# Two chunks per operation for the weighted activations of the late values, in a block with attention and product-key experts

## What is computed

```
def block(args):
    xt, et, gt = args
    u = expert_u[et]
    act = jax.nn.gelu(jnp.einsum('td,tkd->tk', xt, u), approximate=False) * gt
    return jnp.einsum('tk,tkd->td', act, expert_v[et])
```

## Time and profile before

| what | value |
|---|---|
| median of 3 runs | 1699.81 us |
| the profiled execution's own time | 1700.5 us |
| its span, first to last instruction | 1698.6 us |
| mean granted TensorE clock, share of full speed | 0.991 |
| TensorE matmuls busy | 1641.3 us, 97% |
| VectorE busy | 1375.8 us, 81% |
| ScalarE busy | 719.9 us, 42% |
| GpSimd busy | 767.5 us, 45% |
| moved by DMA | 432.17 MB, mean 254 GB/s |

### The profile page before, as it was taken

How to read it: one execution, slowest core, us unless ns; L and a number is a source line. 1 busy time by engine, 2 the same in 40 slices (tenths; PEclk the granted TensorE clock), 3 DMA queues, 4 the chain that set the end, 5 groups by cost and what they waited for, 6 DMA issues and landing times.

```text
span 1698.6 us, 24181 instructions
## 1 busy us (share of the span) xinstructions
PE 1641.3 (97%) x8700; PEld 1441.1 (85%) x8700; DVE 1375.8 (81%) x2835; ACT 719.9 (42%) x1135; POOL 767.5 (45%) x441
## 2 busy tenths in 40 slices
PE   6999999999999999999999889999999999999998
PEld 4677877877899999899999879999999988888886
DVE  7457656676688787999999589888879989888887
ACT  3356546543553534444444333333333344333334
POOL 0222222335356665656554445555555665333331
PEclk9999999999999999999999989999999999999999
DMA  8322242334143432578886999999998999999992
GB/s 331 115 100 87 105 180 88 138 123 149 39 140 116 156 126 96 205 265 340 322 316 225 385 397 378 360 370 360 356 367 328 342 399 398 398 367 376 378 357 100
DMA packets 141676, 432.17 MB, mean 254 GB/s; under 512 B 13584, under 2 KB 58640, under 8 KB 135696
## 3 DMA queue, kind: packets, MB, share of 16 engines
q1 hardware_dynamic: 88592, 265.61, 42.6%
q0 software_dynamic: 41472, 151.01, 23.4%
q10 hardware_dynamic: 11520, 14.42, 2.3%
HBM read 389.31 MB, written 41.68 MB: 254 GB/s over the span
## 4 chain that ended last, share of the span: by engine, by line
PE 68%; DVE 22%; DMA 4%; issue 3%; POOL 1%; ACT 1%; SPq 0%; DVEq 0%; ACTq 0%
PE bank L990 29%; PE bank L934 12%; PE bank L709 10%; DVE hot_j L1732 5%; PE bank L873 4%; DVE hot_i L1728 2%; PE bank L978 2%; DVE rows L1610 2%; DMA rows<-ev,idx 1%; DMA gates<-gates_scratch 1%; PE bank L735 1%; DMA gates_scratch<-stage 1%; DVE arena L1688 1%; PE bank L796 1%; DVE slots L1621 1%
## 5 line engine op out<-in xcount | busy, mean ns | idle before, releaser
L934 PE MATMUL bank<-h_split,u_split 128*128 128x352 f32 x3072 | 518.3, 325 | 8.6 <-DVE u_split L1604 6.9
L934 PEld LDWEIGHTS bank<-h_split,u_split 128*128 128x128 f32 x3072 | 496.6, 189 | 16.5 <-DVE u_split L1604 8.0
L990 PE MATMUL bank<-v_late,a_late 128*128 128x512 f32 x1440 | 326.7, 389 | 1.4 <-DVE a_late L1778 1.4
L990 PEld LDWEIGHTS bank<-v_late,a_late 128*128 128x128 f32 x1440 | 270.2, 188 | 57.7 <-issue 1.6
L609 POOL DMA_INDIRECT rows<-ev,idx x128 | 177.0, 1383 | 219.2 <-DVE row_sum L1719 192.7
L592 POOL TENSOR_TENSOR u_split<-u_raw,u_split 128x1024 fp32r<-128x1024 f32 x72 | 172.8, 2404 | 196.4 <-ACT u_split L1199 196.4
L582 POOL TENSOR_TENSOR block_split<-arena,block_split 128x1024 fp32r<-128x1024 f32 x48 | 118.1, 2464 | 305.6 <-ACT block_split L1054 305.6
L609 POOL DMA_INDIRECT rows<-eu,idx x128 | 182.6, 1427 | 145.4 <-DVE dots L1610 122.3
L990 PE MATMUL bank<-v_split,a_split 128*128 128x512 f32 x864 | 205.6, 392 | 8.6 <-DVE a_split L1778 8.6
L1208 ACT ACTIVATE gelus<-bank 128x352 f32<-128x352 f32 x128 | 59.5, 465 | 324.0 <-PE bank L934 324.0
L990 PEld LDWEIGHTS bank<-v_split,a_split 128*128 128x128 f32 x864 | 162.3, 190 | 39.4 <-issue 8.8
(11 more groups left out here) (281 smaller groups left out, 2406.0 us busy)
## 6 DMA issues: line engine op xcount, KB each, us to landing
u_raw<-euT SPq DMA_DIRECT2D x128, 512.0 KB, 7.8
v_raw<-ev SPq DMA_DIRECT2D x128, 512.0 KB, 7.4
arena<-w_blocks SPq DMA_DIRECT2D x50, 512.0 KB, 9.1
arena<-w_ada SPq DMA_DIRECT2D x12, 2048.0 KB, 8.2
gates_scratch<-stage SPq DMA_DIRECT2D x24, 1024.0 KB, 11.3
gates<-gates_scratch SPq DMA_DIRECT2D x32, 768.0 KB, 10.6
gelu_scratch<-gelus ACTq DMA_DIRECT2D x80, 176.0 KB, 3.4
gelus<-gelu_scratch SPq DMA_DIRECT2D x80, 176.0 KB, 9.4
```

The source lines that it names most:

```text
L934: last = pe.matmul(ps[6 + b][:, 0:TE], us[:, b, wp, k * P:(k + 1) * P], hs[:, xp, k, 0:TE], start=(k == 0 and q == 0), stop=(k == DC - 1 a ...
L990: last = pe.matmul(ps[2 * t + f][:], a[:, ap, t * P:(t + 1) * P], v[:, vp, f * 512:(f + 1) * 512], start=(first and q == 0), stop=True, sk ...
```

## The change

In the late values the multiplication with the gates, the rounding and the low half take two chunks (768 columns) in one operation each: `weights_pair`, `a_high_pair`, `a_low_pair`. `weights` has four slots instead of two. The operations on `v_raw` stay one per chunk, and so do SP's loads and TensorE's matmuls.

The order on VectorE becomes, for each even i: weights_pair(i+2), v_low(i+1), the row sums of chunk i, v_low(i+2), a_low_pair(i+2), the row sums of chunk i+1. On ScalarE it becomes: v_high(i+2), a_high_pair(i+2), v_high(i+3). weights_pair waits for the activations of both chunks, and each pair operation raises its semaphore by 2 when all of it is done.

```diff
-        wgt = carve(2, TD, name="weights")
+        wgt = carve(4, TD, name="weights")
...
-            a_high(NF)
+            def a_high_pair(i):
+
+                sa.wait_ge(w_ready, i + 2)
+                if i >= NF + LATE:
+                    sa.wait_ge(v_done, i - LATE + 2)
+                act_(a_late[:, i % LATE:i % LATE + 2, 0, :], wgt[:, i % 4:i % 4 + 2, :], ACT.Copy).then_inc(a_hi, 2)
+
+            a_high_pair(NF)
             v_high(NF + 1)
-            for i in range(NF, NK):
-                if i + 1 < NK:
-                    a_high(i + 1)
+            for i in range(NF, NK, 2):
                 if i + 2 < NK:
                     v_high(i + 2)
+                    a_high_pair(i + 2)
+                    v_high(i + 3)
...
-            weights(NF)
-            a_low(NF)
-            for i in range(NF, NK):
-                if i + 1 < NK:
-                    weights(i + 1)
-                    v_low(i + 1)
-                    a_low(i + 1)
+            def weights_pair(i):
+
+                if i % 4 == 0:
+                    ve.wait_ge(gt_in[i // 4 % GT], 16 * (i // 4 // GT + 1))
+                for k in (i, i + 1):
+                    ve.wait_ge(gl_in[k % RING], 16 * ((k - NF) // RING + 1))
+                if i >= NF + 4:
+                    ve.wait_ge(a_hi, i - 2)
+                if i < NF + 4:
+                    ve.wait_ge(a_hi, NF)
+                by_64 = dict(n=GROUPS // 16)
+                nv.tensor_tensor(wgt[:, i % 4:i % 4 + 2, :].rearrange("p i (n t) -> p i n t", **by_64),
+                                 gel[:, i % RING:i % RING + 2, :].rearrange("p i (n t) -> p i n t", **by_64),
+                                 gt[i // 4 % GT][:, :, i % 4:i % 4 + 2, :].rearrange("p n i t -> p i n t"), ALU.mult).then_inc(w_ready, 2)
+
+            def a_low_pair(i):
+
+                ve.wait_ge(w_ready, i + 2)
+                ve.wait_ge(a_hi, i + 2)
+                e = i % LATE
+                nv.tensor_tensor(a_late[:, e:e + 2, 1, :], wgt[:, i % 4:i % 4 + 2, :], a_late[:, e:e + 2, 0, :].bitcast(F32),
+                                 ALU.subtract).then_inc(a_split, 2)
+
+            weights_pair(NF)
+            a_low_pair(NF)
+            for i in range(NF, NK, 2):
+                if i + 2 < NK:
+                    weights_pair(i + 2)
+                v_low(i + 1)
                 for k in range(accs_before(i), accs_before(i + 1)):
+                    add_row(k)
+                if i + 2 < NK:
+                    v_low(i + 2)
+                    a_low_pair(i + 2)
+                for k in range(accs_before(i + 1), accs_before(i + 2)):
                     add_row(k)
```

## The result

The kernel became slower: 1764.84 us, the median of 4 runs (1762.38 to 1776.09), against 1700.28 us before, also the median of 4. The ratio is 1.0391, interval 1.0371 to 1.0411. The forecast was 1732 us with a range up to 1785; so the direction and the range held, but the loss was 65 us instead of 32, twice as much.

A forecast was written before the change was run, and what follows sets the result against it. TensorE bounds the late values before the change; afterwards a loop through gelu loads makes four chunks 18.1 us instead of 16.34, 17 times, 30 us, plus 1.1 us for the first pair: 1732 us, range up to 1785 us.

The forecast's parts named there:

- What bounds the kernel: Late values: one unbroken piece of TensorE work, 323.98 us, four chunks 16.34 us; the transfers, at 400 GB/s, have no slack.
- merged operations: VectorE and ScalarE in the late values: merging saves 5.6 us and 8 us, both under TensorE's 324 us, priced at nothing.
- first pair: Start of the late values: longer weights, rounding and low half start TensorE 1.1 us later, its wait growing to 2.5 us.
- The loop: Late values: weights_pair waits for a gelu load issued only after the previous turn's v_low, so each turn includes its landing.
- The turn without gates: VectorE turn with no gate load: 6.1 us alone, 7.4 us with one row fetch, upper bound 10.8 us.
- the prediction's floor: Turn without gates: VectorE's own work of two weights-sized pair operations, two v_low-sized ones and 2.4 row sums, 6.9 us.
- The turn with a gate load: 17 VectorE turns whose gelu load follows a gate load: 8.0 us alone, 10.7 us with two row fetches.
- The choice between the bounds: Turn lengths taken nearer the lone landing than the crowded one, because a loop awaiting its own loads leaves no older ones queued.
- The upper bound: Turn with a gate load at the crowded landing of 9.6 us: 12.6 us.
- TensorE as the bound: Rival for the late values: two turns stay under 16.34 us, only 1.1 us is lost, 1702 us; chance 0.24.
- As crowded as before: Rival for the late values: landings stay crowded, four chunks take 23.4 us, 1822 us in all; chance 0.17.
- TensorE's clock: Late values: idling some 2 us per four chunks might lower the clock, costing 1.7 us; nothing added, put into upper end.

## Why the prediction was right in its mechanism and half its size

- **What bounds the kernel, merged operations, first pair.** Right. The merged operations took the predicted 0.95 and 0.84 us and were worth nothing. TensorE's first late matmul waited 2.52 us, against 1.43 before (both rows are in the section on the result): 1.1 us, as worked out.
- **The loop.** Right, and shown: it goes with SP's order alone, it stays without merging, it shrinks when two links change places.
- **The turn without gates.** Predicted 7.4 us, measured 7.25, but partly by luck. The prediction added a landing with one fetch. In 12 of the 16 turns VectorE didn't wait for gelus at all, and its own work set the length, 6.4 us with two row sums and 7.8 us with three: the prediction's floor of 6.9 us.
- **The turn with a gate load.** This is the term that failed: "I take two: 8.0 + 2.6 = 10.7 us". It measured 12.55 us. By the runs, the loads alone land 1.2 us later than bytes at 400 GB/s make them (6.3 against 5.1 us), and the fetches, 2.8 of them in the mean instead of two, add 3.1 us instead of 2.6; the remaining 0.1 us or so is not resolved. Four chunks take 19.8 us instead of 18.1, and 17 x 3.45 = 59 us are lost instead of 30.
- **The choice between the bounds.** "Nearer to the lone landing than to the crowded ones" was wrong. The reason given holds for SP's own loads, since without the fetches the landings behind gates stay within 5.7 to 6.7 us, but not for the fetches, which bunch around the gate loads. The upper bound, 12.6 us, would have been the better value for the gate turn, but that it fits so well is luck: its landing of 9.6 us is one of 17 behind gate loads before the change, which took 8.6 to 14.7 us and 10.9 in the mean, so it was no upper bound either.
- **Rivals.** TensorE as the bound fell. The 7.5 us that the prediction quotes for this rival rests on a figure that the Trainium skill (DMA: Bandwidth & Descriptors, Anatomy of one DMA) gives for transfers issued from GpSimd; these loads are issued by SP, and the gate turns took 12.55 us. "As crowded as before" held in part for the landings behind gates (9.4 us in the mean, 10.9 before), less for the others (6.5 us, 9.0 before), so 1822 us was too much.
- **TensorE's clock.** The idle was foretold as some 2 us per four chunks; it came in gaps of up to 6 us, and the granted clock fell to 0.85 to 0.98 in every stretch of 40 us from 1360 us on. Its 21 us didn't add to the time: VectorE, which sets the loop's pace, waited 101.9 us for gelus and 1.0 us for anything that hangs on TensorE. A run that holds the clock up wasn't tried.

## What to carry to other kernels

When the order on one engine changes, follow every in-order queue that waits for it: here SP's loads stood behind v_low, and moving v_low behind weights made each weights wait for a load that is issued only after the v_low behind the weights before it, so the landing came into every turn. A prefetch has the lead that its last releaser gives it, counted in turns of the loop, and not the number of buffers. When such a loop must be sized, take several landings behind the same loads and not one, and count what the other queue can issue meanwhile: here the loop's own rhythm put most of the fetches beside the gate loads.

## What the runs showed of the hardware beyond that

- A gate load of 768 KB in pieces of 1 KB landed in 6.2 us, one in pieces of 6 KB, from another tensor, in 5.3 us (medians of 17), both without other traffic than SP's own loads.
- Nine gate turns lasted 9.2 to 12.4 us, with 0.5 to 2.7 fetches moved beside the same loads, and eight lasted 13.9 to 15.4 us, with 3.0 to 4.0: how the transfers of two queues met went with landings from 6.0 to 12.3 us.
- Merging VectorE operations of 384 columns into 768 cost no rate on the strided pair views: 0.952 us (low half) and 0.959 us (weights) for 768 against 0.55 us for 384.
